# Stationary operands moved from 64 to 128 bytes behind the moving operands, modulo 256

## The reference

```python
for l in range(2):
    x = x + 0.5 * swiglu(rms_norm(x, g1), w_gate, w_up, w_down)      # D_FF = 2816
    z = rms_norm(x, g) @ w_in                                         # 1024 x 2816
    # differential attention (4 heads), a 31-tap and a 3-tap causal convolution
    x = x + concat([o_att, o_cc, o_sc]) @ w_out
    hq = rms_norm(x, gx) @ xa_wq;  kv = rms_norm(mem, gm) @ xa_wkv    # 256 memory tokens
    x = x + softmax(hq @ mk.T / 16) @ mv @ xa_wo                      # 4 heads of 256
    x = x + 0.5 * swiglu(rms_norm(x, g2), w_gate, w_up, w_down)
return rms_norm(x, g_final)
```

## Time and profile before

| | |
|---|---|
| time, median of 3 runs (lowest to highest) | 1122.81 us (1122.33 to 1123.4) |
| the profiled execution | 1120.5 us, its span 1118.8 us |
| TensorE (PE) busy in the span | 1111.8 us, 99%, 8828 matmuls |
| weight loads (PEld) | 1070.9 us, 96% |
| VectorE, ScalarE | 830.9 us (74%), 628.5 us (56%) |
| DMA | 211.25 MB, mean 189 GB/s |
| granted TensorE clock | 1.0 of full speed |

### The profile page before, as it was taken

The page is one execution under the profiler, slowest core; times in us unless marked ns, Lnnn a source line. Parts: engine busy times, 40 slices in busy tenths (PEclk is TensorE's granted clock), DMA queues, the critical chain, the costliest instruction groups (busy, mean ns, idle before and its releaser), DMA issues.

```text
span 1118.8 us, 20774 instructions
## 1 busy us (share of the span) xinstructions
PE 1111.8 (99%) x8828; PEld 1070.9 (96%) x8828; DVE 830.9 (74%) x1162; ACT 628.5 (56%) x871; POOL 18.0 (2%) x42
## 2 busy tenths in 40 slices
PE   9999999999999999999999999999999999999998
PEld 8999999999899999999999999999999999888886
DVE  7766667999978775655686675589998878866764
ACT  7554555557765654444574554474767756644454
POOL 1000000010000000000000000000100000000000
PEclk9999999999999999999999999999999999999999
DMA  8965654555454376555647655546546444666561
GB/s 273 324 213 190 218 170 177 189 189 178 162 170 170 117 238 218 184 192 190 207 156 247 221 180 194 193 151 204 174 152 224 156 148 151 201 199 203 187 195 51
DMA packets 69932, 211.25 MB, mean 189 GB/s; under 512 B 5072, under 2 KB 28240, under 8 KB 65232
## 3 DMA queue, kind: packets, MB, share of 16 engines
q1 hardware_dynamic: 68864, 209.19, 55.4%
q10 hardware_dynamic: 976, 0.73, 0.2%
HBM read 208.85 MB, written 1.05 MB: 188 GB/s over the span
## 4 chain that ended last, share of the span: by engine, by line
PE 99%; DMA 0%; ACT 0%; DVE 0%; issue 0%; ACTq 0%; DVEq 0%
PE G L1886 10%; PE G L1888 10%; PE G L1887 10%; PE G L1912 8%; PE D L1717 8%; PE D L1725 8%; PE D L1718 8%; PE G L1920 4%; PE D L1828 2%; PE D L1829 2%; PE D L1830 2%; PE D L1764 2%; PE D L1763 2%; PE D L1762 2%; PE G L1829 2%; PE G L1828 2%
## 5 line engine op out<-in xcount | busy, mean ns | idle before, releaser
L1097 DVE TENSOR_TENSOR w_lo<-w_raw,w_hi 128x2048 fp32r<-128x2048 f32 (+3 forms) x260 | 452.7, 1747 | 106.2 <-ACT w_hi L674 105.0
L674 ACT ACTIVATE w_hi<-w_raw 128x2048 fp32r<-128x2048 f32 (+3 forms) x260 | 383.3, 1481 | 163.5 <-PE G L1888 112.1
L1886 PE MATMUL G<-a,w_hi 128*128 128x256 f32 x990 | 273.8, 277 | 0.3 <-DVE w_lo L1097 0.3
L1888 PE MATMUL G<-a,w_lo 128*128 128x256 f32 x990 | 273.3, 276 | 0.0
L1887 PE MATMUL G<-a,w_hi 128*128 128x256 f32 x990 | 273.3, 276 | 0.0
L1886 PEld LDWEIGHTS G<-a,w_hi 128*128 128x128 f32 x990 | 185.8, 188 | 0.7 <-DVE w_lo L1097 0.5
L1887 PEld LDWEIGHTS G<-a,w_hi 128*128 128x128 f32 x990 | 185.9, 188 | 0.0
L1888 PEld LDWEIGHTS G<-a,w_lo 128*128 128x128 f32 x990 | 185.9, 188 | 0.0
L1717 PE MATMUL D<-hT_hi,w_hi 128*128 128x256 f32 x528 | 145.7, 276 | 0.0
L1718 PE MATMUL D<-hT_lo,w_hi 128*128 128x256 f32 x528 | 145.7, 276 | 0.0
L1725 PE MATMUL D<-hT_hi,w_lo 128*128 128x256 f32 x528 | 145.7, 276 | 0.0
(11 more groups left out here) (309 smaller groups left out, 2086.1 us busy)
## 6 DMA issues: line engine op xcount, KB each, us to landing
w_raw<-w_dram SPq DMA_DIRECT2D x116, 1024.0 KB, 5.0
w_raw<-w_dram SPq DMA_DIRECT2D x151, 512.0 KB, 5.2
m_raw<-memT_dram SPq DMA_DIRECT2D x2, 1024.0 KB, 9.2
w_raw<-w_dram SPq DMA_DIRECT2D x6, 256.0 KB, 6.0
w_raw<-w_dram SPq DMA_DIRECT2D x8, 128.0 KB, 4.1
vx<-mem_dram SPq DMA_DIRECT2D x1, 1024.0 KB, 11.8
out_dram<-vx SPq DMA_DIRECT2D x3, 256.0 KB, 2.2
m_raw<-x_dram SPq DMA_DIRECT2D x2, 256.0 KB, 4.4
```

Of the source, the lines that this page charges most:

```text
L674: A(w_hi[:, part_hi(i)], w_raw[:, part(i)], ACT.Copy).then_inc(s_hi, 1)
L1097: V.tensor_tensor(w_lo[:, part_lo(i)], w_raw[:, part(i)], w_hi[:, part_hi(i)].bitcast(F32), ALU.subtract).then_inc(s_lo, 1)
L1886: M(out, whi[:, w], a_hi[:, k, :], start=(k, u) == (0, 0), stop=False, skip_group_check=True)
L1888: last = M(out, wlo[:, w], a_hi[:, k, :], start=False, stop=k == KD - 1, skip_group_check=True)
```

## The change

`SHIFT` goes from 16 floats (64 bytes) to 32 floats (128 bytes). So every shifted block of `w_hi` and `w_lo`, and `hq_hi`/`hq_lo`, lies 128 bytes behind the moving operands modulo 256, where it lay 64 bytes behind. The room `m` grows by 16 floats with it, and the filler `line_const` of 16 floats goes, so that everything behind it stays where it was. `vx_hi`, `vx_lo` and `mean_r` stay at 64 bytes. No instruction is added, removed or moved on any engine.

```diff
 LINE = 64
-SHIFT = 16
+SHIFT = 32
 GROUP = 1024
 RING_APART = RING + LINE * (RING // GROUP)
@@
         m, hq = halves(0), halves(SHIFT)
         m_hi, m_lo = m[:, :, 0, :], m[:, :, 1, :]
-        sb("line_const", [P, 16])
         const = sb("const", [P, NCONST])
```

## The result

The changed kernel takes 1157.87 us, the median of four runs (1157.6 to 1158.48), against 1122.57 us (1122.31 to 1123.4) of the kernel before on the same chip: a ratio of 1.0314 with a 95% interval of [1.0302, 1.0326], so 3.1% slower. The profiled execution took 1157.6 us, its span 1155.9 us, 37.1 us more than before. The range of the prediction ended at 1146. What came is, in shape, its first rival, a slow pace everywhere, priced at 1156.

A forecast was written before the change was run, and what follows sets the result against it. TensorE, busy 1111.8 of 1118.8 us, was taken to bound the kernel through its matmul paces. All terms were 0 except -0.7 us for slow stretches: 1120.5 to 1119.8 profiled, median 2.3 above, forecast 1122.1; range 1119.5 to 1146.

The forecast's parts named there:

- first rival: All shifted 256-column products fall to the slow pace for good at 128 bytes: 35 us, so 1156; chance 0.15.
- Instructions, waits, splits and switches: No instruction or wait changes; weight splits on ScalarE/VectorE; last FFN's distance switches, 0.8 us either way: each term 0.
- The pace of the shifted products: Matmuls during which a shifted weight or `hq` is loaded: 113.3 ns kept at 128 bytes, term 0.
- The sign: L1886's mean at 281 ns and some 1613 matmuls in the 45 to 235 us window would mean the slow pace.
- 113.3 is found at 0 and at 64 bytes alike: 512-column products at phase 0 run at half of 226.7 per 256 columns, so 113.3 holds at both distances.
- The transposes show that loads at 128 bytes are not slowed: Sixteen 128-column transposes at L1779, operand `x` 128 bytes behind the identity, run at 109 ns.
- The slow stretches: Six stretches after transposes or other 128-column products lose 1.5 us at the slow pace; half taken as gain, -0.7 us.
- The count: Number of matmuls during which a weight or `hq` at the new phase is loaded: 7466, 7.5 us per ns.
- The quick pace entered less often: 113.3 exists, but long FFN stretches may start slow and stay slow: one gives 1130, three 1146; chance 0.20.
- A lower floor: Pace of the shifted 256-column products could reach the transposes' 109 ns: 32 us less, 1091; chance 0.05.
- The second rule's 109.2: Skill's back-to-back gap, N/2.4 + 2.5 ns, for 256 columns; no 256-column stream in the trace reached it.
- That the distance does nothing: No effect anywhere, also in the slow stretches: 1122.8; no separate chance, included in the forecast's own 0.47.

The follow-up runs named there:

- the second experiment: Changed kernel's weights at 128 bytes, with moving operands x, a, hT and m also 64 bytes later, so distance is 64 again: 1135.14 us, ratio 1.0118.
- first two experiments: First: kernel before with every buffer 64 bytes later, all distances kept, 1122.09 us, ratio 1.000; the other is the second experiment.
- run 1336: Not a run label: "run" is a verb here, and 1336 counts products in a row at 117 to 119 ns in the second experiment, 1135.14 us.

## Why the prediction was wrong

*Instructions, waits, splits and switches* were right: the same counts and waits, 1912 and 2291 ns for the splits, 391 and 389 for the wide products.

*The pace of the shifted products* is the step that failed. It took 113.3 "for the long stretches, for two reasons"; the pace at 128 bytes is 118.67, and the term is +37.4 us in the traces instead of 0. The sign that the prediction had named for this, a mean of 281 ns for L1886, came as 282. Both reasons were readings of another width of product:
- "113.3 is found at 0 and at 64 bytes alike". It was found at 0 for 512 columns only. At 256 columns and distance 0 the pace is 120.0, and at 512 columns and distance 64 it is 233.3, half of which is 116.7. The two widths want different distances, so that neither tells of the other. An argument for this is that a load, 188 ns in the record, is longer than a 256-column product's pace and shorter than a 512-column one's, and so meets more of the moving reads; no run measured that.
- "The transposes show that loads at 128 bytes are not slowed". In the changed kernel they still run at 109 while the stream at the same distance takes 118.7. Nor do they change in the second experiment, where `x` lies at 192 from the identity: 109 again. From 113.3 ns for 256 columns more (226.7 less 113.3), 128 moving columns need some 57 of the 109 ns, an estimate; so the moving side has time to spare there, and such a product can't show what loads and moving reads do to each other.

*The slow stretches*: the term of -0.7 has no place left, since all streams of this width became slow. Their loss at the old distance was 2.1 us from start to start, not the 1.5 that six stretches gave.

*The count* was 7466 and is 7417. The rival's sum, with 118.0 from a stretch of 45 matmuls, gave 1156; with the pace of a long stream, 118.67, it gives 1120.5 + 37.4 = 1157.9 for the profiled execution, which took 1157.6. That this is also the median, 1157.87, is luck: the profiled execution before lay 2.3 us under its median and the one after only 0.3, so that the medians grew by 35.3 us and the spans by 37.1. The mechanism that I gave 0.15, a slow pace everywhere, was right, and its price 2 us low; it took the pace for the one of 118 that exists at 64, and it is another. Evidence for it was in the earlier trace rows: a second pace at the same places modulo 256 suggests that what counts is how loads and moving reads fall against each other in time, and then their distance may count too. I used it to argue that the distance doesn't set the pace "alone", and then gave the distance no weight.

*The other rivals.* The quick pace entered less often is real, but at 64 and 192 bytes: the first FFN of the second experiment, and the three of the kernel at 192. It was not what happened at 128, where none of the three long windows is quick. A lower floor, 109, appeared at none of six distances; 113.3 is the best seen. The second rule's 109.2 was not tested by this: The Trainium skill, "TensorE: Matmul & The Clock Gate", section "Back-to-back issue gap", gives that formula for an isolated matmul, and the prediction held it against streams with a load for each. That the distance does nothing is refuted by the same weights, moved to 0, at 1167.64 us. With it falls, for this kernel, what the first rule would have made of the time: The Trainium skill, "SBUF — State Buffer", section "Who interferes with whom", has the two read ports of TensorE independent of each other; here the same loads and the same moving reads cost 113.3 or 120.0 ns by their distance alone.

**What is shown and what is open.** Shown: the distance modulo 256 between the operand being loaded and the one moving sets the pace, and the absolute place doesn't (first two experiments); one load of three at a bad distance slows the whole stream (the kernel with `w_lo` alone at 128); an FFN pays for its own distance and not for the one ahead of it (the kernel with one FFN at 128). The period is 256 bytes, as far as these kernels tell: 0 and 128 differ, and one stream at 113.3 runs through blocks that `LINE` sets 256 bytes apart modulo 512. Open: what inside TensorE's reads makes it so, what decides at 64 and at 192 bytes whether a stream starts at the quick pace, and why two products with another stationary operand can turn a running stream. That the paces of long streams are 17 x 6.67 = 113.3, 18 x 6.67 = 120.0, 34 x 6.67 = 226.7 and 35 x 6.67 = 233.3 suggests that a product takes a whole number of some step, but nothing here tests it. The paces between are not mixtures of these, product by product: at 192 bytes the steps of the first FFN are 117 to 119 ns, never 113 or 120.

## What to carry to other kernels

When TensorE is busy 99% of the time and waits for nobody, read the pace from start to start (matmuls in a window), not the busy share: it had 3 to 4% in it that no wait shows. Try the distance between stationary and moving operands modulo 256 bytes as a parameter of its own, for each width of product; here 64 for 256 columns and 0 for 512. Judge a distance only by a long stream of the same width, and keep all its loads at the same distance, since one in three spoiled it here. A stream's pace is also a matter of how it was entered, so count matmuls in several windows before a distance is called good or bad.

## What the runs showed of the hardware that was not expected

- The pace of a 256-column product behind a weight load each is 113.3 ns at best and 120.0 at worst, by the distance of two operands in SBUF alone, at a granted clock of 1.00.
- With shapes, lines and operand places the same, a stream at a distance of 64 bytes can run 1336 products at 117.8 (first FFN of the second experiment) or whole FFNs at 113.3 (its later ones).
- Two products with another stationary operand, `mean_r`, turned such a stream from 117.8 to 113.3 twice, without a pause of TensorE; at 96 bytes they turned one from 117.3 to 119.7.
- A distance of 0 lengthens the weight load's record from 188 to 192 ns; 128 doesn't, though its pace is 5.3 ns longer.
